# Differential attention inside its projection and its out product, with the head norms split around their roots

## The chip, the cores and the metric

The kernel runs on one core of one Trainium2 chip. The metric is the device time of one execution in microseconds, as the median of the runs. The engines of the core are TensorE (PE; its weight loads are PEld), VectorE (DVE), ScalarE (ACT), GpSimd (POOL) and SyncE (SP, which issues the DMAs). Each works through its own queue in order, and they meet at semaphores.

## The reference, cut to what matters

Two blocks of two layers are computed on 256 tokens of width 1024. The change lies in one layer, the differential attention of the second block. It has 8 heads with two maps each (16 maps), a norm of each map's query and key, a rotation of their first 16 features, two softmaxes per head of which the second is subtracted, and a norm of each head's result before the out product:

```python
def _diff_attention(h, positions, w_qkv, q_gain, k_gain, lam_q1, lam_k1, lam_q2, lam_k2,
                    subln_gain, w_out, lambda_init):
    ...
    qkv = h @ w_qkv
    q, k, v = jnp.split(qkv, 3, axis=-1)
    q = _rmsnorm(q.reshape(B, S, H, 2, Dh), q_gain)
    k = _rmsnorm(k.reshape(B, S, H, 2, Dh), k_gain)
    v = v.reshape(B, S, H, 2 * Dh)
    ...
    q = _partial_rope(q, cos, sin)
    k = _partial_rope(k, cos, sin)
    ...
        p = jax.nn.softmax(s, axis=-1)
        a = (p[:, :, 0] - lam * p[:, :, 1]).astype(v_t.dtype)
        return jnp.einsum('bhqk,bhkd->bhqd', a, v_t)
    ...
    o = (_rmsnorm(o, subln_gain).astype(jnp.float32) * (1.0 - lambda_init)).astype(h.dtype)
    return o.reshape(B, S, H * 2 * Dh) @ w_out
```

## The kernel before

Eight phases follow each other on the core: mixer "ev", mixture of experts "m0", mixer "od", "m1", mixer "sg", dense feed forward "ff", mixer "da" (the differential attention), "m2". All tensors are float32. A projection is made exact enough by splitting each operand into a high and a low part and adding three products (lines 465 to 467); ScalarE makes the high part of a weight piece (`pj_hi`, line 492), VectorE the low part (`pj_lo`, line 502). The order of the work is written out by hand: each engine's queue is the order in which the functions below call it, and nothing else sorts it.

Phase "da" has four steps before the change.

Projection. The weight `w_qkv` of 1024 x 3072 comes in six pieces of 512 columns, two of queries, two of keys, two of values. A piece is multiplied in four quarters (`project_quarter`) of 12 matmuls. A quarter's place in `pj_hi` and `pj_lo` is free once TensorE has used it (`pj_used`), and the next piece's quarter then fills it: a cast on ScalarE, a subtraction on VectorE, which I call a low part. Token tiles 0 and 1 collect in a pair of PSUM banks, three pairs in turn (`da_pair`).

Head norms. For a query or key piece ScalarE squares the banks (line 2764), and VectorE's `da_heads_vector` sums per map, asks GpSimd for the reciprocal root (`rsqrt_vector`, which asks and at once waits; GpSimd's instruction is line 357) and rotates. Later `da_turn_tensor` transposes the piece's result on TensorE (8 transposes, line 2717), a turn. All of VectorE's queue behind `da_heads_vector`, the next piece's low parts too, stands while it waits for the root.

Units. One unit is one map. TensorE makes its logits (lines 2738, 2739), VectorE masks them and takes the maximum (line 674), ScalarE makes the exponentials (652), TensorE transposes them (632), ScalarE copies them out of PSUM (660), TensorE multiplies by the values (640), VectorE divides and, for every second unit, subtracts the pair and sums squares (681, 2877 to 2884). `attention_tensor` and its two partners run the 16 units as a pipeline of three stages: logits of unit u, transposes of u-1, values of u-2. PSUM banks for logits, transposes and outputs are doubled.

Out product. One norm over all 8 heads (2888, root, 2892), 16 transposes of the mix (574), copies with the gain on VectorE (610), and 32 matmuls of 512 columns (587; the profile shows each as two instructions), 8 for each piece `k` of the out weight and each token tile. The first two stages of this, the norm and the transposes, wait for the last unit (`mix_ready`). While TensorE multiplies, VectorE makes the low parts of the first expert's weights. Then VectorE adds the result to `h` (line 600), and phase "m2" begins.

## Time and profile before

| | |
|---|---|
| median of 3 runs | 2301.13 us (2300.80, 2301.13, 2312.22) |
| the profiled execution | 2296.46 us |
| its span, first to last instruction | 2294.7 us |
| TensorE busy, share of the span | 2137.6 us, 93% |
| VectorE busy | 1745.9 us, 76% |
| ScalarE busy | 1429.3 us, 62% |
| phase "da" from the end of its first piece to its last matmul | 1104.6 to 1255.1 us |

A line of the trace names the engine, the line of the kernel, the operation and "out<-in" by the program's names; "arena" is the tensor that holds most of a phase's intermediate results, "bank" is PSUM. The start of each instruction is in microseconds from the start of the span. A matmul's duration reaches over the start of the next one, since they are pipelined, so what one costs is read from one start to the next.

### The profile page before, as it was taken

Reading aid. Unit: us, or ns where it says so; the run is one execution under the profiler, and the core shown is the slowest. Engines: PE = TensorE matmul, PEld = TensorE weight load, DVE = VectorE, ACT = ScalarE, POOL = GpSimd, SP = SyncE. Lnnn points to the kernel's source line nnn. Section 1 sums busy time; section 2 is a strip of 40 time slices with the busy share of each in tenths; the row PEclk is TensorE's granted clock in tenths of the full one; section 3 lists DMA queues with packets and bytes.
Section 4 is the critical chain, followed back from the end, with each engine's and each line's share of the span. In section 5 each row is a group of like instructions: output and inputs, shape, how many; then the busy total and the mean of one; then the engine's idle time right before and its main releaser. Section 6 shows DMA issues by size and latency. Waiting matters only on the chain.

```text
span 2294.7 us, 31436 instructions
## 1 busy us (share of the span) xinstructions
PE 2137.6 (93%) x9970; PEld 1729.8 (75%) x9970; DVE 1745.9 (76%) x2350; ACT 1429.3 (62%) x1919; POOL 76.3 (3%) x71
## 2 busy tenths in 40 slices
PE   8998997997997998999887799999999999999998
PEld 7965776865775886887764687878878787878786
DVE  4755888646887656555664698989899898989897
ACT  5652775443774543444441587877778787878785
POOL 0001000001000000111100000000000000000000
PEclk9998999997998998999998899999999999999999
DMA  6324883423873544542320698989989898989895
GB/s 248 145 80 192 334 330 142 152 112 152 362 273 119 194 185 187 232 169 96 120 111 1 269 383 318 378 315 381 369 331 376 324 373 323 374 322 376 320 386 207
DMA packets 81400, 577.11 MB, mean 251 GB/s; under 512 B 9392, under 2 KB 9392, under 8 KB 12848
## 3 DMA queue, kind: packets, MB, share of 16 engines
q1 hardware_dynamic: 79744, 570.40, 63.3%
q0 software_dynamic: 1584, 5.77, 0.8%
q8 instruction: 43, 0.70, 0.1%
q14 instruction: 29, 0.24, 0.0%
HBM read 575.08 MB, written 1.05 MB: 251 GB/s over the span
## 4 chain that ended last, share of the span: by engine, by line
PE 77%; DVE 12%; issue 5%; ACT 4%; DMA 1%; POOL 1%; DVEq 0%; SPq 0%; ACTq 0%; POOLq 0%
PE bank L465 22%; PE bank L467 21%; PE bank L466 21%; PE bank L587 2%; PE bank L923 2%; PE bank L1396 2%; DVE h L1754 1%; PE bank L1362 1%; DVE gu_lo L1702 1%; DVE pj_lo L502 1%; DVE dn_lo L1702 1%; PE bank L1435 1%; ACT gu_hi L1531 1%; ACT dn_hi L1539 1%; DVE hidt_lo L1702 1%
## 5 line engine op out<-in xcount | busy, mean ns | idle before, releaser
L1702 DVE TENSOR_TENSOR gu_lo<-ffw_gu,gu_hi 128x1024 fp32r<-128x1024 f32 x620 | 755.3, 1238 | 89.7 <-ACT gu_hi L1531 75.0
L1531 ACT CAST gu_hi<-ffw_gu 128x1024 fp32r<-128x1024 f32 x620 | 648.2, 1053 | 102.0 <-PE bank L467 69.1
L465 PE MATMUL bank<-gu_hi,xg_lo 128*128 128x512 f32 x1152 | 462.5, 401 | 5.8 <-DVE xg_lo L1702 4.7
L467 PE MATMUL bank<-gu_hi,xg_hi 128*128 128x512 f32 x1152 | 451.8, 392 | 0.0
L466 PE MATMUL bank<-gu_lo,xg_hi 128*128 128x512 f32 x1152 | 451.1, 392 | 0.0
L1702 DVE TENSOR_TENSOR dn_lo<-ffw_d,dn_hi 128x1024 fp32r<-128x1024 f32 x299 | 362.7, 1222 | 57.4 <-ACT dn_hi L1539 48.0
L1539 ACT CAST dn_hi<-ffw_d 128x1024 fp32r<-128x1024 f32 x310 | 325.3, 1055 | 95.2 <-PE bank L467 91.5
L465 PE MATMUL bank<-dn_hi,hidt_lo 128*128 128x512 f32 x664 | 264.9, 399 | 29.3 <-DVE hidt_lo L1702 29.3
L467 PE MATMUL bank<-dn_hi,hidt_hi 128*128 128x512 f32 x664 | 259.1, 390 | 0.0
L466 PE MATMUL bank<-dn_lo,hidt_hi 128*128 128x512 f32 x664 | 259.0, 390 | 0.0
L465 PEld LDWEIGHTS bank<-gu_hi,xg_lo 128*128 128x128 f32 x1152 | 217.5, 189 | 48.7 <-DVE xg_lo L1702 5.3
L467 PEld LDWEIGHTS bank<-gu_hi,xg_hi 128*128 128x128 f32 x1152 | 217.2, 189 | 46.2
L466 PEld LDWEIGHTS bank<-gu_lo,xg_hi 128*128 128x128 f32 x1152 | 218.1, 189 | 41.5
L502 DVE TENSOR_TENSOR pj_lo<-pieces,pj_hi 128x1024 fp32r<-128x1024 f32 (+2 forms) x108 | 125.3, 1179 | 69.6 <-ACT pj_hi L492 59.6
L492 ACT CAST pj_hi<-pieces 128x1024 fp32r<-128x1024 f32 (+2 forms) x104 | 104.1, 1011 | 112.4 <-PE bank L467 98.2
L465 PEld LDWEIGHTS bank<-dn_hi,hidt_lo 128*128 128x128 f32 x664 | 124.7, 188 | 64.6 <-DVE hidt_lo L1702 24.1
L465 PE MATMUL bank<-pj_hi,xm_lo 128*128 128x512 f32 (+2 forms) x320 | 129.9, 406 | 21.3 <-DVE xm_lo L447 14.2
L467 PEld LDWEIGHTS bank<-dn_hi,hidt_hi 128*128 128x128 f32 x664 | 124.6, 188 | 26.5
L466 PEld LDWEIGHTS bank<-dn_lo,hidt_hi 128*128 128x128 f32 x664 | 124.8, 188 | 24.0
L1561 ACT CAST hidt_hi<-bank 128x256 fp32r<-128x256 f32 x166 | 61.9, 373 | 124.2 <-PE bank L1362 124.2
L467 PE MATMUL bank<-pj_hi,xm_hi 128*128 128x512 f32 (+2 forms) x320 | 125.9, 394 | 0.0
L466 PE MATMUL bank<-pj_lo,xm_hi 128*128 128x512 f32 (+2 forms) x320 | 125.8, 393 | 0.0
(397 smaller groups left out, 2794.7 us busy)
## 6 DMA issues: line engine op xcount, KB each, us to landing
ffw_gu<-in_gate_up_m SPq DMA_DIRECT2D x288, 1024.0 KB, 6.9
ffw_d<-in_down_m SPq DMA_DIRECT2D x144, 1024.0 KB, 7.5
pieces<-in_pieces SPq DMA_DIRECT2D x70, 1024.0 KB, 7.0
ffw_gu<-in_gate_up_ff SPq DMA_DIRECT2D x22, 1024.0 KB, 6.9
ffw_d<-in_down_ff SPq DMA_DIRECT2D x11, 1024.0 KB, 8.9
pieces<-in_pieces SPq DMA_DIRECT2D x4, 512.0 KB, 8.1
norm_vec<-in_ln_g POOLq DMA_DIRECT2D x4, 512.0 KB, 3.9
norm_vec<-in_ln_b POOLq DMA_DIRECT2D x4, 512.0 KB, 5.2
```

Source lines behind the costliest of these rows:

```text
L465: nc.tensor.matmul(bank, a_lo, b_hi, start=start, stop=False)
L466: nc.tensor.matmul(bank, a_hi, b_lo, start=False, stop=False)
L467: return nc.tensor.matmul(bank, a_hi, b_hi, start=False, stop=stop)
L492: nc.scalar.copy(pj_hi[:, 2 * k:2 * k + 2, 0:cols], piece_ap(g)[:, 2 * k:2 * k + 2, :]).then_inc(sem("pj_hi_ready"), 1)
L502: V.tensor_tensor(pj_lo[:, cs, 0:cols], piece_ap(g)[:, cs, :], pj_hi[:, cs, 0:cols].bitcast(F32), ALU.subtract).then_inc(sem("pj_split"), 1)
L587: last = nc.tensor.matmul(psum[2 * j + half], mixT[:, k, c, j * P:(j + 1) * P], wt[:, c, half * 512:(half + 1) * 512], start=(k == 0 and c ...
L923: last = nc.tensor.matmul(psum[2 * j + half], ev_mixT[:, k, c, TILES[j]], piece_ap(even_out[k])[:, c, half * 512:(half + 1) * 512], start= ...
L1396: last = nc.tensor.matmul(psum[5 + half], pick_t[:, j, :], src[:, j, cols], start=(j == 0 and part == 0), stop=(j == T - 1 and part == 1))
L1531: nc.scalar.copy(gu_hi[:, 2 * k:2 * k + 2, :], ffw_gu[:, blk["slot"], 2 * k:2 * k + 2, :])\
L1539: nc.scalar.copy(dn_hi[:, f, :], ffw_d[:, blk["slot"], f, :]).then_inc(sem("down_hi_ready"), 1)
L1561: nc.scalar.copy(hidT_hi[:, st["par"]].rearrange("p f t -> p (f t)"), psum[2][:, st["par"] * BLK:(st["par"] + 1) * BLK]).then_inc(sem("hid ...
L1702: return V.tensor_tensor(out, x, hi.bitcast(F32), ALU.subtract)
```

## The change

Phase "da" is put in another order. The pieces come as query 0, key 0, value 0, query 1, key 1, value 1, so that maps 0 to 7 are complete after three pieces. Their eight units then run between the quarters of pieces 3 to 5: `da_step_tensor(pe, 0, i)` for i from 0 to 9 behind quarters 12 to 21 (`DA_STEP`), with the stages of the pipeline as before. The turns stand behind quarters 6, 11, 20 and 23 (`DA_TURN`). Units 8 to 15 run after the projection, with the 16 matmuls of the first out piece between them in eight parts of two (`DA_OUT_BEHIND`). The head norm of a piece is in two steps, `da_heads_begin_vector` before the root and `da_heads_end_vector` behind it, with two low parts between them. The norm before the out product is made for heads 0 to 3 and heads 4 to 7 apart, each in two steps too. The projection uses two pairs of banks and not three; units use one bank for the transposes (6) and one for the outputs (7, in halves). Three memsets that stood behind the first head norm stand at the head of VectorE's queue.

```diff
-    da = [("qkv", "tok", columns("l1_da_w_qkv_2", 512 * i, 512 * (i + 1)), 512) for i in range(6)]
+    da = [(("q", "k", "v")[i // 2], "tok", columns("l1_da_w_qkv_2", 512 * i, 512 * (i + 1)), 512) for i in (0, 2, 4, 1, 3, 5)]
...
+    DA_STEP = {12 + i: i for i in range(10)}
...
+    def da_step_tensor(pe, first, i):
+
+        if i < 8:
+            u = first + i
+            for g in range(2):
+                pe.wait_ge(sem(f"turned_read{g}"), DA_TURNED + 2 + first // 4)
+            if i >= 2:
+                pe.wait_ge(sem("at_masked"), DA_U0 + u - 1)
+            q, k, bank = (da_q_odd if u % 2 else da_q_even)[:, u // 2, :], da_kT[:, u // 2, :], psum[4 + u % 2]
+            nc.tensor.matmul(bank[:, 0:P], q[:, 0:P], k[:, 0:P], start=True, stop=True)
+            nc.tensor.matmul(bank[:, P:3 * P], q[:, P:S], k, start=True, stop=True).then_inc(sem("at_logits"), 1)
+        if 1 <= i <= 8:
+            u = first + i - 1
+            pe.wait_ge(sem("at_probs"), DA_U0 + u + 1)
+            if u:
+                pe.wait_ge(sem("at_probst"), DA_U0 + u)
+            for b in range(3):
+                last = nc.tensor.transpose(psum[6][:, b * P:(b + 1) * P], da_probs[:, u % 2, b, :], ident)
+            last.then_inc(sem("at_turned"), 1)
+        if i >= 2:
+            u = first + i - 2
+            pe.wait_ge(sem("at_probst"), DA_U0 + u + 1)
...
+            if u:
+                pe.wait_ge(sem("at_written"), DA_U0 + u)
...
+            last.then_inc(sem("at_outputs"), 1)
...
     def da_tensor(pe):
         t = "da"
-        project_first_tensor(pe, t, da_pair(0))
+        project_first_tensor(pe, t, 0)
         for n in range(1, 6):
...
+            for k in range(4):
+                project_quarter(pe, t, n, k, 2 * (n % 2))
+                at = 4 * n + k
+                if at in DA_STEP:
+                    da_step_tensor(pe, 0, DA_STEP[at])
+                if at in DA_TURN:
+                    da_turn_tensor(pe, DA_TURN[at])
...
+        da_mix_turn_tensor(pe, 0)
+        parts = 0
+        for i in range(10):
+            da_step_tensor(pe, 8, i)
+            for _ in range(DA_OUT_BEHIND.count(i)):
...
+                last = da_out_tensor(0, j, half, cs)
+                parts += 1
+        last.then_inc(sem("out_piece"), 1)
+        da_mix_turn_tensor(pe, 1)
...
+        for j in range(T):
+            for half in range(2):
+                last = da_out_tensor(1, j, half, range(4))
+            last.then_inc(sem("out_tile"), 1)
...
     def da_scalar(act):
...
+            for k in range(4):
+                at = 4 * n + k
+                piece_hi_scalar(act, "da", n + 1, (k,))
+                if k == 3:
+                    da_evacuate_scalar(act, n)
+                if at in DA_STEP:
+                    da_step_scalar(act, 0, DA_STEP[at])
+                if at in DA_TURN:
+                    da_turned_scalar(act, DA_TURN[at])
...
+    def da_heads_begin_vector(dve, n):
...
+        root_ask_vector()
+        da_asked[n] = roots["asked"]
+
+    def da_heads_end_vector(dve, n):
+
+        m = DA_MAPS[DA_ROUND[n]]
+        dve.wait_ge(sem("root_found"), da_asked[n])
...
     def da_vector(dve):
+        vlink(V.memset(da_q_even[64:P], 0.0))
+        vlink(V.memset(da_q_odd[0:64], 0.0))
+        vlink(V.memset(at_sums, 0.0))
         for n in range(6):
...
+            for k in range(4):
+                at = 4 * n + k
+                i = DA_STEP.get(at, -1)
+                if at == 12:
+                    da_values_vector(dve, n - 1)
+                if 0 <= i < 8:
+                    da_mask_vector(dve, i)
+                if k == 0 and n - 1 in DA_ROUND:
+                    da_heads_begin_vector(dve, n - 1)
+                piece_lo_vector(dve, "da", n + 1, (k,))
+                if i >= 2:
+                    da_write_vector(dve, i - 2)
+                if i == 9:
+                    da_norm_begin_vector(0)
+                if k == 1 and n - 1 in DA_ROUND:
+                    da_heads_end_vector(dve, n - 1)
+                if at == 22:
+                    da_norm_end_vector(0)
+                if at in DA_TURN:
+                    da_turned_vector(dve, DA_TURN[at])
+        da_values_vector(dve, 5)
+        da_mixed_vector(dve, 0)
+        for i in range(10):
+            if i < 8:
+                da_mask_vector(dve, 8 + i)
+            if i >= 2:
+                da_write_vector(dve, 6 + i)
+        da_norm_begin_vector(1)
+        da_norm_end_vector(1)
+        da_mixed_vector(dve, 1)
```

VectorE's queue at the end of the first piece, before. L502 is a low part, L2785 and L2787 are the norm before its root, L2793 to L2805 the norm behind it and the rotation, and the memsets clear the halves of the query tensors.

```order
L502 TENSOR_TENSOR pj_lo<-pieces,pj_hi 128x1024 x4
L2785 TENSOR_REDUCE arena<-arena 128x16
L2787 TENSOR_SCALAR arena<-arena 128x16
L2793 TENSOR_SCALAR arena<-arena 128x16
L2802 TENSOR_TENSOR arena<-arena,spare 128x16x8
L2803 TENSOR_TENSOR arena<-arena,spare 128x16x8
L2804 TENSOR_TENSOR arena<-arena,spare 128x256
L2805 TENSOR_TENSOR arena<-arena 128x2x8x16
L2867 MEMSET arena 64x2048
L2868 MEMSET arena 64x2048
L2869 MEMSET small 128x32
L502 TENSOR_TENSOR pj_lo<-pieces,pj_hi 128x1024 x4
```

The same place after the change, where the two steps of the norm are lines 2894, 2896 and 2908 to 2920:

```order
L3031 MEMSET arena 64x2048
L3032 MEMSET arena 64x2048
L3033 MEMSET small 128x32
L502 TENSOR_TENSOR pj_lo<-pieces,pj_hi 128x1024 x4
L2894 TENSOR_REDUCE arena<-arena 128x16
L2896 TENSOR_SCALAR arena<-arena 128x16
L502 TENSOR_TENSOR pj_lo<-pieces,pj_hi 128x1024 x2
L2908 TENSOR_SCALAR arena<-arena 128x16
L2917 TENSOR_TENSOR arena<-arena,spare 128x16x8
L2918 TENSOR_TENSOR arena<-arena,spare 128x16x8
L2919 TENSOR_TENSOR arena<-arena,spare 128x256
L2920 TENSOR_TENSOR arena<-arena 128x2x8x16
```

The memsets now stand ahead of the first low parts, and two low parts stand between the sum and what needs the root.

TensorE's queue where the projection ends and the units begin, before. L465 to L467 belong to a quarter, L2717 is a turn, L2738 and L2739 are a unit's logits, L632 its transposes, L640 its products with the values.

```order
L467 MATMUL bank<-pj_hi,xm_hi 128x512
L2717 MATMUL bank<-ident,arena 128x128 x8
L2738 MATMUL bank<-arena 128x128
L2739 MATMUL bank<-arena 128x256
L2738 MATMUL bank<-arena 128x128
L2739 MATMUL bank<-arena 128x256
L632 MATMUL bank<-ident,arena 128x128 x3
L2738 MATMUL bank<-arena 128x128
L2739 MATMUL bank<-arena 128x256
L632 MATMUL bank<-ident,arena 128x128 x3
L640 MATMUL bank<-arena 128x128 x3
```

After the change, TensorE's queue between quarters 13 and 14 (from the last three matmuls of quarter 13), where L2746 are the transposes:

```order
L465 MATMUL bank<-pj_hi,xm_lo 128x512
L466 MATMUL bank<-pj_lo,xm_hi 128x512
L467 MATMUL bank<-pj_hi,xm_hi 128x512
L2738 MATMUL bank<-arena 128x128
L2739 MATMUL bank<-arena 128x256
L2746 MATMUL bank<-ident,arena 128x128 x3
L2759 MATMUL bank<-arena 128x128 x3
L465 MATMUL bank<-pj_hi,xm_lo 128x512
L466 MATMUL bank<-pj_lo,xm_hi 128x512
```

And after the projection, where L2769 are the 8 transposes of half the mix, L2759 the products with the values, and each L2776 is a matmul of the out product:

```order
L2725 MATMUL bank<-ident,arena 128x128 x8
L2769 MATMUL bank<-ident,arena 128x128 x8
L2738 MATMUL bank<-arena 128x128
L2739 MATMUL bank<-arena 128x256
L2776 MATMUL bank<-pieces,arena 128x512 x2
L2738 MATMUL bank<-arena 128x128
L2739 MATMUL bank<-arena 128x256
L2746 MATMUL bank<-ident,arena 128x128 x3
L2776 MATMUL bank<-pieces,arena 128x512 x2
L2738 MATMUL bank<-arena 128x128
L2739 MATMUL bank<-arena 128x256
L2746 MATMUL bank<-ident,arena 128x128 x3
L2759 MATMUL bank<-arena 128x128 x3
L2776 MATMUL bank<-pieces,arena 128x512 x2
```

Units 0 to 7 stand singly between quarters, each step behind 12 matmuls, and units 8 to 15 have parts of the out product between them, which stood behind all units before.

## Rows read from the trace of the kernel before

**Rows 1.** The page: the chain that ended last, its shares by engine.
```profile
PE 77%; DVE 12%; issue 5%; ACT 4%; DMA 1%; POOL 1%; DVEq 0%; SPq 0%; ACTq 0%; POOLq 0%
```

**Rows 2.** Stretches: length, busy (x) of PE, PEld, DVE, ACT, POOL, PEclk, DMA, GB/s.
```profile
1104.60:1174.20 69.60, 61.85 (x273) 50.35 (x272) 44.67 (x59) 30.62 (x38) 11.60 (x4) 0.95 0.42 154
1174.20:1216.80 42.60, 29.61 (x208) 24.56 (x208) 29.75 (x136) 22.20 (x81) 0.00 (x0) 1.00 0.11 46
1216.80:1222.70 5.90, 0.03 (x1) 0.03 (x1) 2.63 (x4) 0.05 (x1) 2.89 (x1) 0.62 0.00 0
1222.70:1226.60 3.90, 3.90 (x17) 3.44 (x18) 2.08 (x3) 3.84 (x4) 0.00 (x0) 0.50 0.02 4
1226.60:1255.10 28.50, 28.50 (x67) 12.61 (x67) 9.91 (x14) 0.00 (x0) 0.56 (x1) 0.97 0.00 0
```

**Rows 3.** Waits, 1104.6 to 1260: who waited for whom: us, times, longest.
```profile
PE bank L632 <- ACT arena L652: 10.6, 9, 1.5
...
PE bank L465 <- DVE pj_lo L502: 6.8, 3, 4.0
DVE arena L2793 <- POOL arena L357: 6.2, 2, 3.1
```

**Rows 4.** Timeline around the second weight piece: start, us, engine, line, [idle before <-releaser].
```profile
1101.66 3.92 DVE L502 TENSOR_TENSOR pj_lo<-pieces,pj_hi 128x1024 fp32r<-128x1024 f32 x3 [2.30 <-ACT pj_hi L492]
...
1108.68 2.91 POOL L357 TENSOR_TENSOR arena<-arena,small 128x16 f32<-128x16 f32 x1 [13.80 <-DVEq L362]
...
1113.97 1.76 DVE L2867 MEMSET arena<- 64x2048 f32 x1 [0.60 <-DVE arena L2805]
...
1119.46 0.79 PE L465 MATMUL bank<-pj_hi,xm_lo 128*128 128x512 f32 x1 [3.99 <-DVE pj_lo L502]
```

**Rows 5.** Timeline, TensorE alone, one attention unit that waits for nothing.
```profile
1186.29 0.39 PE L2738 MATMUL bank<-arena 128*128 128x128 f32 x2
1186.51 0.60 PE L2739 MATMUL bank<-arena 128*128 128x256 f32 x2
1186.94 0.49 PE L632 MATMUL bank<-ident,arena 128*128 128x128 f32 x3
1187.27 0.83 PE L640 MATMUL bank<-arena 128*128 128x128 f32 x6
1187.94 0.39 PE L2738 MATMUL bank<-arena 128*128 128x128 f32 x2
```

**Rows 6.** Timeline, TensorE alone: a quarter's ends, and the transposes of a turn.
```profile
1109.64 0.39 PE L467 MATMUL bank<-pj_hi,xm_hi 128*128 128x512 f32 x1
...
1112.36 0.39 PE L467 MATMUL bank<-pj_hi,xm_hi 128*128 128x512 f32 x1
...
1131.91 1.03 PE L2717 MATMUL bank<-ident,arena 128*128 128x128 f32 x8
1132.70 0.48 PE L465 MATMUL bank<-pj_hi,xm_lo 128*128 128x512 f32 x1
```

**Rows 7.** Busy time of the out product's line alone, 1234 to 1254.
```profile
1234.00:1254.00 20.00, 20.00 (x48) 8.76 (x48) 1.00 0.00 0
```

**Rows 8.** VectorE's groups by line, 1104.6 to 1174.1: xcount, busy us, mean ns.
```profile
L502 DVE TENSOR_TENSOR pj_lo<-pieces,pj_hi 128x1024 fp32r<-128x1024 f32 x18 | 21.2, 1222 | 1.5 <-ACT pj_hi L492 0.7 <-DVE arena L2805 0.2
```

**Rows 9.** GpSimd's root line: xcount: duration ns min/median/max, start us, forms.
```profile
L357 POOL TENSOR_TENSOR small<-small x20: 545/554/1042, 160.9 to 1260.5; 128x1 f32<-128x1 f32 x18, 128x4 f32<-128x4 f32 x1, 128x2 f32<-128x2 f32 x1
L357 POOL TENSOR_TENSOR arena<-arena,small x5: 2894/2896/2907, 1108.7 to 1217.2; 128x16 f32<-128x16 f32 x5
```

**Rows 10.** Timeline: two places where VectorE and GpSimd work side by side.
```profile
892.53 0.55 POOL L357 TENSOR_TENSOR small<-small 128x1 f32<-128x1 f32 x1 [5.61 <-DVEq L362]
892.54 1.25 DVE L1702 TENSOR_TENSOR xt_lo<-xT,xt_hi 128x1024 fp32r<-128x1024 f32 x1
...
1022.54 2.40 POOL L1684 TENSOR_TENSOR dn_lo<-ffw_d,dn_hi 128x1024 fp32r<-128x1024 f32 x1 [14.43 <-ACT dn_hi L1539]
...
1023.86 2.17 DVE L1702 TENSOR_TENSOR gu_lo<-ffw_gu,gu_hi 128x1024 fp32r<-128x1024 f32 x1 [1.49 <-ACT gu_hi L1531]
```

More of the change, by code:

```diff
@@ new lines, in da_mix_turn_tensor, with da_out_tensor @@
+    def da_mix_turn_tensor(pe, k):
+        pe.wait_ge(sem("mix_ready"), 4 + k)
+        for b in range(2):
+            for i in range(4):
+                c, j = 2 * b + i // 2, i % 2
+                last = nc.tensor.transpose(psum[4 * k + b][:, i * P:(i + 1) * P],
+                                           da_mix[:, j, 512 * k:512 * (k + 1)].rearrange("t (p c) -> t c p", c=4)[:, c, :], ident)
+            last.then_inc(sem("mixt_turned"), 1)
+    def da_out_tensor(k, j, half, cs):
+        for c in cs:
+            last = nc.tensor.matmul(psum[2 * j + half], da_mixT[:, k, c, TILES[j]],
+                                    piece_ap(da_out[k])[:, c, half * 512:(half + 1) * 512],
+                                    start=(k == 0 and c == 0), stop=(k == 1 and c == 3))
+        return last
@@ L2734, in da_tensor @@
[L2734 to L2742 removed]
+                read_wait(pe, t, 0, n - 1)
@@ new lines, in da_norm_begin_vector, with da_norm_end_vector @@
+    def da_norm_begin_vector(k):
+        vlink(V.tensor_scalar(da_hs_flat[k], da_hs_flat[k], RMS_EPS, None, ALU.add))
+        root_ask_vector()
+    def da_norm_end_vector(k):
+        root_wait_vector()
+        for j in range(T):
+            y = da_mix[:, j, 512 * k:512 * (k + 1)].rearrange("p (h d) -> p h d", d=P)
+            vlink(V.scalar_tensor_tensor(out=y, in0=y, scalar=1.0 - LAMBDA_INIT, in1=over(da_hs[:, k, j, :], 2, P),
+                                         op0=ALU.mult, op1=ALU.mult), *([sem("mix_ready")] if j else []))
@@ new lines, in da_turned_vector, with da_values_vector @@
+    def da_turned_vector(dve, o):
+        dve.wait_ge(sem("da_qk_turned"), 2 * o + 2)
+        for dst, src, gain in da_turned_parts(DA_MAPS[o], 1):
+            last = V.tensor_scalar(dst, src, gain, None, ALU.mult)
+        last.then_inc(sem("turned_read1"), 1)
+    def da_values_vector(dve, n):
+        full_wait(dve, "da", 1, n)
+        vlink(V.tensor_scalar(da_v[:, 1, 512 * (n // 3):512 * (n // 3 + 1)], psum[2 * (n % 2) + 1], rstd[:, 1:2], None,
+                              ALU.mult), sem("bank1_read"))
```

223 lines of the change are left out of this document (122 added, 101 removed).

## Prediction

> **What bounds the kernel now.** I read four things, in this order. First the chain that ended last, by engine [rows 1]: 77% of the span is TensorE, so what shortens the time is work or idle time on TensorE's queue. Second, busy time by stretch of the phase that the change touches [rows 2]. The reader is to see that TensorE works 61.85 of 69.6 us in the projection, 29.61 of 42.6 us in the units, nothing in the 5.9 us of the norm, and that its clock is 0.50 in the 3.9 us of transposes behind that idle time. The five stretches make 150.5 us, from 1104.6 (the end of the first weight piece) to 1255.1 (the last matmul). Third, who waits for whom [rows 3]: in the units TensorE waits for ScalarE's exponentials, nine waits that the profile names with 10.6 us in all; in the projection it waits for VectorE's low parts, 6.8 us, and VectorE stands for a root, 3.1 us each time. Fourth, the timeline of the second piece [rows 4]: the root runs from 1108.68 for 2.91 us, then come the rotation and, from 1113.97, the memsets, and TensorE has idled 3.99 us when its low part is there at 1119.46. VectorE is no bound here: 44.67 of 69.6 and 29.75 of 42.6 us. The idle time comes from the order of the queues.
>
> **Prices.** A quarter is 12 matmuls, from 1109.64 to 1112.36, 2.72 us [rows 6]. A turn moves the next matmul from 1131.91 to 1132.70, 0.8 us [rows 6]. A unit that waits for nothing costs TensorE 1.65 us, from its logits at 1186.29 to the next at 1187.94: 0.65 logits, 0.33 transposes, 0.67 values [rows 5]. The same unit took 42.6 / 16 = 2.66 us as the units stood [rows 2]. The out product's row counts 48 instructions in 20 us at full clock and 64 (two for each of 32 matmuls) fill 28.5 us at 0.97 [rows 7, 2]: 0.417 to 0.445 each; I take 0.43, so 0.86 a matmul and 1.7 for a part of two.
>
> **The sum, from the end of the first piece.** I walk the new queues in their order with these prices.
>
> Projection. 20 quarters, 54.4. Four turns, 3.2. Units 0 to 7 now lie between quarters, 8 x 1.65 = 13.2 on TensorE. What each needs of VectorE and ScalarE was asked for a whole slot (2.72 + 1.65 = 4.4 us) earlier, and a unit's work there is 29.75 / 16 = 1.86 and 22.20 / 16 = 1.39 us [rows 2] beside a low part of 1.22 [rows 8], so it is hidden; without that cover a slot would cost the 1.0 us more (2.66 - 1.65) that it cost before. A low part is made a piece ahead of its use, which is four slots: no wait either. Waits that stay: the two memsets of 1.76 us with their gaps of some 0.5 take 4.1 us where VectorE idled 2.30 [rows 4], so the first low part ends near 1104.8 and TensorE waits 0.3. The turn of query 0: VectorE makes the second of two low parts after the second quarter (1104.9 + 5.4 = 1110.3, then ScalarE's cast, put at a low part's 1.22 [rows 8], and the low part, 2.4), then the rotation, 1.8 as from the root's end at 1111.6 to the memset's idle time of 0.60 before 1113.97 [rows 4], ready at 1114.5 to 1114.9; TensorE comes at 1113.1 and waits 1.8. The other turns have more room; between 0 and 3 x 1.8 I take 0.9, near the lower end, since two of them stand two quarters and more behind their rotation. One short stretch at the lower clock after it, 0.7. Projection with eight units: 54.4 + 3.2 + 13.2 + 3.0 + 0.7 = 74.5.
>
> Between. A wait of 0.6 (an estimate, the width of one multiplication of half the mix) for the first half's norm, whose root of 8 columns lies beside other work, and 8 transposes, 0.9, as a turn: 1.5.
>
> Second units and first out piece. Step 0: 0.65 logits, 1.4 until VectorE has copied the transposed half (two copies of 0.69, as 2.08 for three [rows 2]), a part 1.7. Step 1: 0.65 + 0.33 + 1.7. Steps 2 to 4: 1.65 + 1.7 = 3.35 each, more than the 2.66 of the loop through the other engines, so TensorE sets them: 10.1. Steps 5 to 7 have no part: 2.66 each, 8.0. Step 8: 1.0 + 1.7 and 0.7, as the loop still runs through the other engines. Step 9: 0.67 + 3.4. In all 32.1. The eight units and the first out piece alone took 21.3 + 14.2: this place gives 3.4 us only, for two thirds of the idle time of a unit is not covered by a part.
>
> Tail. Before, 5.9 us lay between the last unit and the transposes [rows 2]. The root has 8 columns; 4 took 1.04 and 16 took 2.90 [rows 9], so between these, I take 1.7 and save 1.2. The two multiplications have half the width, 1.1 less. With the last unit's own division and squares (1.9, an estimate; a whole unit is 1.86 on average) it makes 5.5 to 6, of which the last two parts cover 3.4: 2.4. Eight transposes at the lower clock, half of 3.9, are 1.95, the copy behind them 1.35, 16 matmuls 13.7, and 1.2 for the lower clock at their start, as before. 20.6.
>
> Hand-offs that such a sum leaves out, 0.8. Total 74.5 + 1.5 + 32.1 + 20.6 + 0.8 = 129.5, against 150.5: **21 us less**. The queues of SyncE and GpSimd gain no DMA and one root; a piece is asked for when the low parts two before it are done, and slots that grow longer give it more time. ScalarE loads as many activation tables in the new list of instructions as in the old. What follows in phase m2 waits for this phase's end and moves with it. The profiled execution took 2296.46 us, 1.8 more than its span, and would take 2275.5; the median of the runs is 4.7 above it, so I predict 2280.0.
>
> **A rule against it.** The split norm puts a root of 2.90 us beside low parts. Where GpSimd subtracted 1024 columns from 1022.54 for 2.40 us, VectorE's low part, begun at 1023.86, took 2.17 us instead of 1.22: it stood until GpSimd was done. Beside a root of 0.55 us at 892.53, however, one took 1.25, begun 0.01 later [rows 10]. If the four long roots did block as the subtraction did, the low part behind each would start up to 2.9 us later, of which the wait for its quarter hides a part; only where a turn follows soon does it count. Ahead of the first turn the two low parts would end at 1112.8 and 1113.9 (the root's end at 1111.6, then 1.22 and 1.1) and the rotation at 1115.9, 1.1 later; the other turns, with more room, I put at 0.6 together. That is 1.7 us, so 2281.7. I give it 0.12. The Trainium skill, page "SBUF — State Buffer", section "SBUF: two separate sides", states that the port pair that VectorE and GpSimd share is an exclusive lock held for the whole instruction, so that the other fully blocks when a VectorE operation with two SBUF inputs meets one of GpSimd. By that rule the time is 2281.7. The subtraction's rows agree with it, the short root's do not.
>
> **Rivals.**
> - The queues' order costs what it saves: each of the ten slots and eight later steps waits for a hand-off, because masks stand behind low parts and exponentials behind casts. For it: nine such waits in the units now, up to 1.5 us. Against it: the slot of 4.4 us. At 0.5 us in 18 places the gain is 12, time 2289; at 1.0, which is the old cost, 3 and 2298. Chance 0.15 for the first and 0.04 for the second.
> - Slower: TensorE's clock. If the mix of short matmuls and waits let it fall to the lower of its levels (1.2 GHz) from the first unit on, units 0 to 7 (13.2), the ten quarters between them (27.2), units 8 to 15 (13.2) and the parts (13.7) would cost twice, up to 67 more. It decides from 21 us of such work at half clock on, where the gain is gone. For it: 0.50 behind the idle 5.9 us. Against it: 1.00 through all units, with TensorE busy 29.61 of 42.6, less than it will be [rows 2]. Half of the second group at half clock gives 2293; all of it and the slots give 2347. Chance of an end slower than before 0.02.
> - The change doesn't do what it says, since the phase behind waits for something else than this phase (a weight that lands at a fixed time): within 0.5% of before, 2301. Against it: DMA share is 0.00 behind 1216.8 [rows 2], so nothing is under way that it could wait for. Chance 0.02.
>
> **How the numbers follow.** Forecast (75 to 80 quarters and units hidden, 18 to 24 us gained) 0.65, the lock 0.12, hand-offs 0.15 and 0.04, clock 0.02, nothing 0.02. A difference of 0.5%, 11.5 us, is about what a measurement of this kernel can tell from none. Faster by more than that: 0.65 + 0.12 + 0.15 = 0.92; same 0.04 + 0.02; slower 0.02. The range is 2272 to 2289: its low end has the turns free of waits (2.7), no lower clock in the tail (2.2) and a tail of 1 us less, and 2 us for the spread of the runs; its high end the first case of the hand-offs.
>
> **What the profile will show.** The five stretches' total falls from 150.5 to about 130. TensorE's idle time up to the end of the projection is below 5 us, the largest piece before the first turn; the waits for low parts are gone; the root lies beside a low part, and if that low part takes 1.22 the lock is wrong. Quarters with a unit start 4.4 us apart. In the second group five steps are 3.4 us apart and three 2.7. Before the last transposes there is one wait of 2 to 3 us, and the clock is at 0.50 in them. Wrong it would be with waits for exponentials in every slot, or with a granted clock below 0.9 over the whole stage.

## Result and profile after

| | before | after |
|---|---|---|
| median of 5 runs | 2301.13 us (2300.49 to 2312.22) | 2284.39 us (2279.54 to 2285.40) |
| the profiled execution, its span | 2296.46, 2294.7 us | 2285.40, 2283.7 us |
| TensorE busy | 2137.6 us, 93% | 2142.7 us, 94% |
| end of the first piece to the last matmul | 150.5 us | 131.9 us |

The ratio of the times is 0.9921, 95% interval [0.9907, 0.9934]: 18.2 us less by the ratio. 21 were predicted; 2284.4 lies in the range. The page's lines of busy time and of the chain by engine, which answer to [rows 1]:

```profile
PE 2142.7 (94%) x9970; PEld 1734.1 (76%) x9970; DVE 1748.5 (77%) x2353; ACT 1429.6 (63%) x1919; POOL 77.7 (3%) x72
...
PE 78%; DVE 11%; issue 5%; ACT 4%; DMA 1%; DVEq 0%; POOL 0%; SPq 0%; ACTq 0%; POOLq 0%
```

The phase from the end of its first piece on, cut at the places where the prediction's sum was cut: projection with units 0 to 7, the first transposes of the mix, second units with parts, wait and last transposes with their copy, last 16 matmuls. The columns are those of [rows 2], busy time of TensorE, its weight loads, VectorE, ScalarE and GpSimd, then clock, DMA share and GB/s:

```profile
1110.14:1187.99 77.85, 73.97 (x376) 61.87 (x376) 57.79 (x127) 41.75 (x78) 14.27 (x5) 0.98 0.37 137
1187.99:1189.60 1.61, 1.04 (x10) 1.07 (x10) 1.46 (x3) 0.29 (x1) 0.00 (x0) 1.00 0.82 285
1189.60:1220.98 31.38, 28.15 (x138) 18.19 (x136) 16.79 (x72) 10.89 (x40) 1.13 (x1) 1.00 0.12 50
1220.98:1225.43 4.45, 1.52 (x9) 1.14 (x9) 2.91 (x5) 2.41 (x3) 0.50 (x1) 0.81 0.00 0
1225.43:1241.97 16.54, 16.54 (x34) 7.24 (x35) 9.03 (x12) 1.48 (x2) 0.56 (x1) 0.84 0.00 1
```

TensorE now has 73.97 us of work in 77.85, where it had 61.85 in 69.6. The clock column reads 0.81 and 0.84 in the last two stretches; part of the 2.4 us by which 131.9 misses the prediction's 129.5 lies there. TensorE's waits up to 1188, and those behind it; they answer to [rows 3]:

```profile
PE bank L2725 <- DVEq L296: 3.1, 3, 2.4
PE bank L465 <- DVE pj_lo L502: 0.8, 1, 0.8
...
PE bank L2769 <- DVEq L296: 2.6, 2, 2.1
PE bank L2746 <- ACT arena L2845: 2.2, 3, 1.1
PE bank L2776 <- issue: 1.0, 1, 1.0
PE bank L2776 <- DVE arena L3027: 0.9, 1, 0.9
```

The nine waits for exponentials (10.6 us) and the three for low parts (6.8 us) of before are gone; one of 0.8 for a low part, behind the memsets, is left. The 2.2 us at L2746 are new in kind: L2845 is ScalarE's copy that frees the one bank of the transposes, and TensorE waits for it in three steps, all without a part in front (1209.21, 1212.20 and 1213.76). Between quarters no wait of a unit is on the list. TensorE's timeline shows the slots, by the first logits of three units that follow each other in the projection, and then the steps of the second group, two with a part and two without:

```profile
1153.62 0.38 PE L2738 MATMUL bank<-arena 128*128 128x128 f32 x2
...
1158.02 0.38 PE L2738 MATMUL bank<-arena 128*128 128x128 f32 x2
...
1162.42 0.38 PE L2738 MATMUL bank<-arena 128*128 128x128 f32 x2
...
1199.32 0.39 PE L2738 MATMUL bank<-arena 128*128 128x128 f32 x2
...
1202.69 0.38 PE L2738 MATMUL bank<-arena 128*128 128x128 f32 x2
...
1206.07 0.38 PE L2738 MATMUL bank<-arena 128*128 128x128 f32 x2
1207.72 0.39 PE L2738 MATMUL bank<-arena 128*128 128x128 f32 x2
...
1210.24 0.39 PE L2738 MATMUL bank<-arena 128*128 128x128 f32 x2
```

Slots are 4.40 us apart (4.4 predicted), steps with a part 3.37 (3.35), and the steps without one 1.65 and then 2.52 (2.66: the first of them lives on the lead that the parts had given the other engines).

The first turn is where most was missed. TensorE's last matmul before it, the turn's eight transposes, and the matmuls behind:

```profile
1119.00 0.39 PE L467 MATMUL bank<-pj_hi,xm_hi 128*128 128x512 f32 x1
1121.78 1.97 PE L2725 MATMUL bank<-ident,arena 128*128 128x128 f32 x8 [2.39 <-DVEq L296]
1123.40 0.78 PE L465 MATMUL bank<-pj_hi,xm_lo 128*128 128x512 f32 x1
...
1124.40 0.58 PE L467 MATMUL bank<-pj_hi,xm_hi 128*128 128x512 f32 x1
1124.81 0.40 PE L465 MATMUL bank<-pj_hi,xm_lo 128*128 128x512 f32 x1
```

It waits 2.39 us instead of 1.8, and then the matmuls start 0.43 apart instead of 0.23 until 1124.8: the lower level of the clock. Why it waits longer stands on VectorE and GpSimd. First VectorE's low parts beside the first two roots, then GpSimd's roots:

```profile
1115.89 1.23 DVE L502 TENSOR_TENSOR pj_lo<-pieces,pj_hi 128x1024 fp32r<-128x1024 f32 x1 [0.15 <-DVE arena L2896]
...
1131.23 1.28 DVE L502 TENSOR_TENSOR pj_lo<-pieces,pj_hi 128x1024 fp32r<-128x1024 f32 x1
```

```profile
1115.94 3.94 POOL L357 TENSOR_TENSOR arena<-arena,small 128x16 f32<-128x16 f32 x1 [15.44 <-DVEq L362]
1131.22 2.90 POOL L357 TENSOR_TENSOR arena<-arena,small 128x16 f32<-128x16 f32 x1 [11.34 <-DVEq L362]
...
1183.45 1.63 POOL L357 TENSOR_TENSOR arena<-arena,small 128x8 f32<-128x8 f32 x1 [2.97 <-DVEq L362]
```

The second root began 0.01 us before its low part, and both ran at their length (2.90; 1.28 for 1.22). The first began 0.05 us behind its low part and took 3.94, 1.04 more; the rotation stood until 1119.9 for it. So one engine did hold the other up here, but the other way round than in the prediction's rival; root_first tests it.

**Outside the stretch.** The phase's first matmul stood at 1088.7 us before and at 1094.3 after, though nothing ahead of it was changed, and from the last addition to `h` to the end of the span it was 1039.7 and 1041.7. Over all profiles shown below these two lengths lie between 1088.6 and 1097.1, and 1038.9 and 1043.2, with no order by kernel. The two profiled executions are also an unequal pair: that of before, 2296.46 us, is below all five timed ones, and that of the changed kernel, 2285.40, is the slowest of its five. So the experiments are compared by the phase itself, from its first matmul to the start of VectorE's addition of token tile 1 to `h` (166.4 before, 147.7 after), and the whole by the timed ratio.

### The profile page after: what moved, and what is told of

It is laid out like the page before. It is cut to its first block, busy times and chain, and to the rows that moved or that the text cites. A ratio compares the mean times of both kernels' runs of the same rounds, so it can differ in the third digit from the quotient of the medians.

```text
span 2283.7 us, 31475 instructions
## 1 busy us (share of the span) xinstructions
PE 2142.7 (94%) x9970; PEld 1734.1 (76%) x9970; DVE 1748.5 (77%) x2353; ACT 1429.6 (63%) x1919; POOL 77.7 (3%) x72
## 4 chain that ended last, share of the span: by engine, by line
PE 78%; DVE 11%; issue 5%; ACT 4%; DMA 1%; DVEq 0%; POOL 0%; SPq 0%; ACTq 0%; POOLq 0%
PE bank L465 22%; PE bank L467 21%; PE bank L466 21%; PE bank L923 2%; PE bank L1396 2%; DVE h L1754 1%; PE bank L1362 1%; PE bank L587 1%; PE bank L2776 1%; DVE gu_lo L1702 1%; DVE dn_lo L1702 1%; DVE pj_lo L502 1%; PE bank L1435 1%; ACT gu_hi L1531 1%; ACT dn_hi L1539 1%
## 5 line engine op out<-in xcount | busy, mean ns | idle before, releaser
L465 PE MATMUL bank<-gu_hi,xg_lo 128*128 128x512 f32 x1152 | 462.9, 402 | 5.0 <-DVE xg_lo L1702 4.5
L467 PE MATMUL bank<-gu_hi,xg_hi 128*128 128x512 f32 x1152 | 452.2, 393 | 0.0
L465 PE MATMUL bank<-dn_hi,hidt_lo 128*128 128x512 f32 x664 | 265.7, 400 | 29.2 <-DVE hidt_lo L1702 29.2
L467 PE MATMUL bank<-dn_hi,hidt_hi 128*128 128x512 f32 x664 | 259.6, 391 | 0.0
L465 PEld LDWEIGHTS bank<-gu_hi,xg_lo 128*128 128x128 f32 x1152 | 217.6, 189 | 48.5 <-DVE xg_lo L1702 5.3
L467 PEld LDWEIGHTS bank<-gu_hi,xg_hi 128*128 128x128 f32 x1152 | 217.4, 189 | 46.4
L502 DVE TENSOR_TENSOR pj_lo<-pieces,pj_hi 128x1024 fp32r<-128x1024 f32 (+2 forms) x108 | 126.1, 1180 | 74.2 <-ACT pj_hi L492 64.5
L465 PEld LDWEIGHTS bank<-dn_hi,hidt_lo 128*128 128x128 f32 x664 | 125.1, 188 | 64.7 <-DVE hidt_lo L1702 24.1
L467 PEld LDWEIGHTS bank<-dn_hi,hidt_hi 128*128 128x128 f32 x664 | 125.0, 188 | 26.7
L465 PE MATMUL bank<-pj_hi,xm_lo 128*128 128x512 f32 (+2 forms) x320 | 130.8, 409 | 15.3 <-DVE xm_lo L447 14.2
L467 PE MATMUL bank<-pj_hi,xm_hi 128*128 128x512 f32 (+2 forms) x320 | 125.9, 394 | 0.0
```

The costliest lines, as they stand in the source:

```text
L465: nc.tensor.matmul(bank, a_lo, b_hi, start=start, stop=False)
L467: return nc.tensor.matmul(bank, a_hi, b_hi, start=False, stop=stop)
L502: V.tensor_tensor(pj_lo[:, cs, 0:cols], piece_ap(g)[:, cs, :], pj_hi[:, cs, 0:cols].bitcast(F32), ALU.subtract).then_inc(sem("pj_split"), 1)
```

## Experiments

The phase in four parts, us, from starts in TensorE's timeline: from the phase's first matmul to the second turn, to the mix's first transposes, to its last ones, to the addition to `h`. Ratios are to the kernel before; where two intervals overlap, only the profile tells the kernels apart, and it is one execution. Timed executions of one kernel lie up to 11.8 us apart (parts_single, 2274.20 to 2285.98), the slower at a lower granted clock (0.965 against 0.969 and 0.970), and where the others lost it isn't recorded. The profile of root_first is the fastest of its four, that of parts_last the slowest of its four (2291.97, with two at 2283).

| kernel | to 2nd turn | to mix | to last | to `h` | phase | ratio, 95% |
|---|---|---|---|---|---|---|
| changed | 44.1 | 50.2 | 34.5 | 19.0 | 147.7 | 0.9921 [0.9907, 0.9934] |
| after_again | 44.1 | 50.2 | 34.5 | 19.0 | 147.7 | 0.9922 [0.9901, 0.9942] |
| norms_whole | 41.0 | 65.3 | 34.7 | 17.9 | 158.9 | 0.9958 [0.9942, 0.9973] |
| units_behind | 43.7 | 64.2 | 35.1 | 16.2 | 159.2 | 0.9978 [0.9966, 0.9989] |
| parts_last | 44.2 | 50.2 | 41.0 | 16.1 | 151.5 | 0.9926 [0.9903, 0.9949] |
| root_first | 41.7 | 50.2 | 34.5 | 16.2 | 142.6 | 0.9894 [0.9873, 0.9915] |
| memsets_gpsimd | 42.3 | 50.2 | 34.5 | 17.9 | 144.8 | 0.9909 [0.9896, 0.9923] |
| turn_later | 40.1 | 50.2 | 34.5 | 19.2 | 144.0 | 0.9906 [0.9891, 0.9921] |
| parts_four | 44.1 | 50.2 | 34.5 | 16.1 | 144.9 | 0.9908 [0.9893, 0.9923] |
| filled_wait | 44.1 | 50.2 | 34.5 | 16.2 | 145.0 | 0.9902 [0.9887, 0.9917] |
| parts_single | 43.7 | 50.1 | 31.4 | 16.1 | 141.4 | 0.9889 [0.9866, 0.9913] |
| all_three | 38.9 | 50.2 | 31.4 | 16.1 | 136.6 | 0.9872 [0.9850, 0.9894] |

A trap lies in the first column. Up to the second turn units_behind and parts_single run the same instructions as the changed kernel, but from the first to the last matmul start of the first piece they took 18.57 and 18.55 us, where the changed kernel and six others with the same instructions there took 15.44 to 15.56 in eight profiles. The first piece in the changed kernel, then in parts_single:

```profile
1094.30:1110.14 15.84, 13.82 (x56) 10.97 (x56) 11.18 (x19) 4.39 (x5) 1.11 (x2) 0.90 0.16 68
```

```profile
1092.26:1111.20 18.94, 16.92 (x57) 13.46 (x58) 12.85 (x20) 4.38 (x5) 1.11 (x2) 0.75 0.14 58
```

The clock is 0.90 and 0.75. The 3.1 us come back in part, since the low parts are then in time and the root comes first (see root_first), which leaves 43.7 for 44.1. So a difference of a microsecond or two in that column can be the clock's and not the edit's.

### norms_whole: the split of the head norms undone

```diff
 if k == 0 and n - 1 in DA_ROUND:
     da_heads_begin_vector(dve, n - 1)
+    da_heads_end_vector(dve, n - 1)
...
-if k == 1 and n - 1 in DA_ROUND:
-    da_heads_end_vector(dve, n - 1)
```

> The head norm of a piece back in one step: behind the root's request VectorE waits for the root and rotates, before any low part; all else as in the changed kernel, whose stretch from the end of the first piece (1110.14) to the last matmul (1242.0) is 131.9 us. Theory (the split carries part of the gain, because in a slot of 4.4 us VectorE has 1.22 of low part and 1.86 of the unit to do, and a stand of 2.9 for the root with 1.8 of rotation doesn't fit beside them): the two norms that lie among the units make TensorE wait 4 to 5 us each, the stretch grows by 8 to 10, to about 141, ratio to the kernel before 0.996. Rival (low parts are made a piece ahead, so the stand is covered and the split is worth nothing): 132 to 134, ratio 0.992 to 0.993.

The theory's ratio and its waits; the phase grew by 11.2 us, a little above its 8 to 10. One of the two waits stands on TensorE, and what VectorE did meanwhile:

```profile
1165.98 1.62 PE L2759 MATMUL bank<-arena 128*128 128x128 f32 x6 [4.56 <-DVEq L296]
1167.25 0.77 PE L465 MATMUL bank<-pj_hi,xm_lo 128*128 128x512 f32 x1
```

```profile
1162.12 0.17 DVE L2908 TENSOR_SCALAR arena<-arena 128x16 f32<-128x16 f32 x1 [3.06 <-POOL arena L357]
...
1164.01 1.23 DVE L502 TENSOR_TENSOR pj_lo<-pieces,pj_hi 128x1024 fp32r<-128x1024 f32 x1
...
1165.35 0.42 DVE L2985 TENSOR_TENSOR arena<-bank,small 128x256 f32<-128x256 f32 x1
```

TensorE waits 4.56 us (and 4.34 at the other norm) for the division of a unit's output, which frees the bank and stands in VectorE's queue behind root, rotation and low part. The stretch to the mix grew by 15.1: 8.9 in these two waits, 1.1 at the first logits, most of the rest at the lower clock behind them (1.62 for a group that takes 0.83). Without the split 11.2 of the phase's 18.7 us are gone, and about half of the gain by the ratio. Ahead of the slots, though, the whole norm costs nothing (41.0 against 44.1).

### units_behind: no units between the quarters

```diff
-DA_STEP = {12 + i: i for i in range(10)}
+DA_STEP = {}
...
+for i in range(10):
+    da_step_tensor(pe, 0, i)
 da_mix_turn_tensor(pe, 0)
```

> Units 0 to 7 run behind the projection and not between its quarters; the norm of heads 0 to 3 then stands open behind them too. All else as in the changed kernel. Theory (a unit costs TensorE 1.65 us between quarters and 2.66 in a row): 8 x 1.0 = 8 us, and some 6 us for the norm that nothing covers any more: the stretch of 131.9 grows to 146, ratio 0.998. Rival (the hand-offs cost in the slots what they cost in a row, the gain is from the norms and parts): growth by the norm's 6 us alone, 138, ratio 0.995.

ScalarE's and VectorE's steps, and the norm of heads 0 to 3, move behind the projection too. From the second turn on, with the last part left out, it is 99.3 against 84.7 us, 14.6 more: the theory's 14, and far from the rival's 6. The whole phase grew by 11.5, since the last part ran at full clock here (16.2 for 19.0). Of TensorE's groups in 1174 to 1202, the transposes of a unit waited 5.7 us for exponentials and copies, and those of the mix 5.5 for the norm:

```profile
L2744 PE MATMUL bank<-ident,arena 128*128 128x128 f32 x24 | 4.2, 282 | 5.7 <-ACT arena L2845 4.4 <-ACT arena L2837 1.2
...
L2767 PE MATMUL bank<-ident,arena 128*128 128x128 f32 x1 | 0.5, 489 | 5.5 <-DVEq L296 5.5
```

### parts_last: the first out piece behind all units

```diff
-DA_OUT_BEHIND = (0, 1, 2, 3, 4, 8, 9, 9)
+DA_OUT_BEHIND = (9, 9, 9, 9, 9, 9, 9, 9)
```

> All eight parts of the first out piece behind step 9 of the second units, none between them. Theory (a part between units fills about 1 us of idle time of a step, while idle time before the last transposes costs twice, as wait and as lower clock behind it): five parts cost 1.7 instead of 0.7, 5.0 more; the wait of 2.1 us before the last transposes goes, and with it the lower clock in them and in the last 16 matmuls (0.6 and 2.7). The stretch stays within 1.5 us of 131.9, ratio 0.992. Rival (the clock's loss at the end isn't due to the wait): 134.5 to 135, ratio 0.993, granted clock behind the parts about 0.8 as now.

Half right. The last stretch fell from 19.0 to 16.1, at full clock, as the theory has it; but the one before grew by 6.5, and the sum by 3.7, where the theory allowed 1.5. The clock was lost in two other places instead, behind a wait of 2.03 us in the first steps and behind waits of 1.89 and 0.37 in the last (the first two rows); behind the parts it was 1.00 (the third), so the rival falls:

```profile
1193.00:1197.00 4.00, 1.97 (x11) 1.55 (x10) 2.60 (x10) 1.92 (x9) 0.00 (x0) 0.87 0.81 338
1211.00:1218.00 7.00, 5.18 (x25) 4.69 (x26) 2.97 (x14) 2.19 (x8) 0.00 (x0) 0.65 0.01 2
...
1234.50:1248.60 14.10, 14.04 (x35) 6.42 (x36) 9.11 (x13) 0.00 (x0) 0.56 (x1) 1.00 0.00 0
```

The timed ratio can't tell it from the changed kernel, and this profile is the slowest of its four executions, so what a kernel with all parts last costs as a rule stays open.

### root_first: the first root begins ahead of the low part

```diff
 root_ask_vector()
+if n == 0:
+    vlink(V.memset(rope_both, 0.0))
```

> One memset of 128x256 on VectorE between the request of the first head norm's root and the low part behind it, so that the root begins before the low part and not 0.05 us behind it. Theory (a 128x16 root holds no low part up, but waits for one that began earlier: 3.94 instead of 2.90 us): the root takes 2.90, the low part beside it 1.28, and TensorE's wait before the first turn falls from 2.39 to about 1.6. Rival (this root is long for another reason, such as GpSimd's 15 us without work): it takes 3.9 again and the wait stays 2.4.

GpSimd, and VectorE beside it:

```profile
1110.20 2.91 POOL L357 TENSOR_TENSOR arena<-arena,small 128x16 f32<-128x16 f32 x1 [15.42 <-DVEq L362]
```

```profile
1110.24 0.27 DVE L2900 MEMSET arena<- 128x256 f32 x1 [0.24 <-DVE arena L2896]
1110.54 1.22 DVE L502 TENSOR_TENSOR pj_lo<-pieces,pj_hi 128x1024 fp32r<-128x1024 f32 x1
1112.10 1.22 DVE L502 TENSOR_TENSOR pj_lo<-pieces,pj_hi 128x1024 fp32r<-128x1024 f32 x1 [0.34 <-ACT pj_hi L492]
```

The root takes 2.91 behind the same 15.4 us without work, so the rival falls; the low part inside it and the one that begins inside it take 1.22 each. All profiles agree: in the six where the first root began 0.05 or 0.06 us behind a low part it took 3.94, in the five where it began 0.28 us or more ahead of it, 2.91. Two of these five, units_behind and parts_single, have no edit there. TensorE's wait is 1.46 instead of 2.39. Behind it the turn took no half clock, so the stretch to the second turn fell by 2.4 and not by 0.9. The last stretch fell too, by 2.7, with the same wait of 2.06 us before it, which nobody expected; see below.

### memsets_gpsimd, turn_later: the first turn's two waits

```diff
+if phase == 6:
+    pool.wait_ge(sem("root_found"), roots["answered"])
+    pool.memset(da_q_even[64:P], 0.0).then_inc(sem("da_zeroed"), 1)
+    pool.wait_ge(sem("da_zeroed"), 1)
+    pool.memset(da_q_odd[0:64], 0.0).then_inc(sem("da_zeroed"), 1)
+    pool.wait_ge(sem("da_zeroed"), 2)
...
-vlink(V.memset(da_q_even[64:P], 0.0))
-vlink(V.memset(da_q_odd[0:64], 0.0))
```

> The two large memsets on GpSimd, at the head of its part of the phase, instead of VectorE. Theory: VectorE's first low part is in time, TensorE's wait of 0.79 us before the second piece is gone, the stretch of 131.9 falls by 0.8 and the stage starts no later. The first root still waits about 1 us if a low part begins first. Rival (GpSimd's memsets hold VectorE's subtractions for the last xm_lo up, as its 1024-column subtraction did): TensorE's wait in the first piece grows by 1 us or more and nothing is gained.

The wait of 0.79 is gone and VectorE isn't held up: GpSimd's second memset ran from 1103.02 for 1.80, and VectorE's two subtractions for `xm_lo`, begun at 1104.25, took 1.29 for both, as without it. The low part here came 0.33 us behind the root, which took 2.91, and the first turn waited 1.45. Against that a lower clock in the first piece cost about 1.4, since without it the stretch would be root_first's 41.7 less 0.8, and it was 42.3.

```diff
-DA_TURN = {6: 0, 11: 1, 20: 2, 23: 3}
+DA_TURN = {7: 0, 11: 1, 20: 2, 23: 3}
```

> The first turn stands behind quarter 7 instead of 6. Theory (its wait of 2.39 us is for the rotation, which is ready 1121.7, before quarter 7 would end, and the half clock in the turn and the quarter behind it comes from that wait): the wait goes, the eight transposes take 0.95 instead of 1.62, the quarter 2.72 instead of 3.2; the stretch falls by 3.0 to 3.6, to about 128.6. Rival (VectorE's later copy pushes the next norm and the wait comes back before the second turn): the second turn waits 2 us instead of 0.44 and less than 1.5 us is gained.

To the second turn 4.0 us less, a little over the theory; the second turn's wait is 0.44 as it was, so the rival falls.

### parts_four, filled_wait: the clock at the end

```diff
-DA_OUT_BEHIND = (0, 1, 2, 3, 4, 8, 9, 9)
+DA_OUT_BEHIND = (0, 1, 2, 3, 9, 9, 9, 9)
```

> Parts behind steps 0, 1, 2, 3, 9, 9, 9, 9 instead of 0, 1, 2, 3, 4, 8, 9, 9. Theory: 6.9 us of parts cover the last unit's division, the norm's root and the multiplications (5.5 us), so that TensorE doesn't idle before the last transposes and its clock stays at the full level: the part taken from step 4 costs 1.0 more, the wait of 2.06 goes, and the lower clock's 3.3 us (0.6 in the transposes, 2.7 in the last 16 matmuls) too; the stretch falls by 3 to 4.5, to 128. Rival (the clock falls at the end of the stage whatever TensorE did before): a fall of 1.0 only, granted clock about 0.8 in the last 16 matmuls.

```diff
 last.then_inc(sem("out_piece"), 1)
+for _ in range(2):
+    nc.tensor.matmul(psum[6], da_mixT[:, 0, 0, TILES[0]], piece_ap(da_out[0])[:, 0, 0:512], start=True, stop=True)
 da_mix_turn_tensor(pe, 1)
+nc.tensor.matmul(psum[6], da_mixT[:, 0, 0, TILES[0]], piece_ap(da_out[0])[:, 0, 0:512], start=True, stop=True)
```

> Three matmuls of 512 columns whose result nobody reads are added: two in the wait before the last eight transposes, one in the wait for their copy (added work, nothing of the result depends on it). Theory (the clock at the end is lost through TensorE's 2 us without work): the granted clock stays 1.00, the transposes take 0.95 instead of 1.52, the last 16 matmuls 13.7 instead of 16.4, and the stretch falls by about 3, though work was added. Rival (the clock is lost for another reason): the stretch stays at 131.9 or grows by 0 to 0.5.

Both theories fit, with 2.8 and 2.7 us less (parts_four just below its bound of 3), but each rests on one profile, and two of the kernels that keep the wait kept the clock as well (root_first, units_behind). What carries it is the count: with a wait of 2.06 five of seven profiles lost the clock behind it, without one none of five did. The timed executions agree in kind: clock 0.969 to 0.970 in parts_four and 0.968 to 0.970 in filled_wait, against 0.965 to 0.970 in the changed kernel. The last stretch of filled_wait, with one of its three added matmuls in it, and that of turn_later, which has the wait of 2.06 before it:

```profile
1224.84:1241.07 16.23, 16.10 (x44) 7.64 (x45) 10.45 (x15) 3.86 (x4) 0.56 (x1) 1.00 0.00 0
```

```profile
1221.20:1240.40 19.20, 18.21 (x42) 8.50 (x43) 10.46 (x14) 3.87 (x4) 0.56 (x1) 0.82 0.00 0
```

Same stretch, clock 1.00 and 0.82. In parts_four the stretch before stayed 34.5: the wait that it saved is what the part taken from step 4 costs. All of its gain is clock.

### after_again, parts_single, all_three

> The changed kernel itself once more, profiled anew beside the next ones. What is meant to be the same: from the first matmul of the phase (which stood at 1094.3) to the second turn 44.1 us, from there to the first transposes of the mix 50.2, to the last ones 34.5. What may differ, if the clock's fall behind a wait of some 2 us is a matter of chance and not of this kernel: the last part, 19.0 us here, was 16.2 in two kernels with the same wait of 2.06 (root_first, units_behind) and 17.9, 17.9 and 19.2 in three others. And the phase's start, 1088.6 to 1097.1 in the profiles so far. Theory: the last part is between 16.2 and 19.2 and the first wait (2.4) costs its half clock again. Rival (the loss belongs to this order of work): 19.0 again within 0.2.

As the rival had it: 18.97 both times, and 44.1 to the second turn. But both profiles are among the slow executions of this kernel (2285.40 is the highest of five, 2287.07 the second highest of six, the lowest is 2279.54), so what the faster ones lost isn't shown.

```diff
-DA_OUT_BEHIND = (0, 1, 2, 3, 4, 8, 9, 9)
+DA_OUT_BEHIND = (0, 1, 2, 3, 4, 5, 6, 7, 8, 9, 9, 9, 9, 9, 9, 9)
...
-j, half, cs = 1 - parts // 4, parts // 2 % 2, ((0, 1), (2, 3))[parts % 2]
+j, half, cs = 1 - parts // 8, parts // 4 % 2, (parts % 4,)
```

> The first out piece in sixteen parts of one matmul instead of eight of two: one behind each of steps 0 to 8, seven behind step 9. Theory (a step of 2.66 us has 1.0 us without work and a part of one matmul is 0.86, so it costs nothing, where a part of two costs 0.7; seven matmuls, 6.0 us, cover the last unit's way to the transposes): from the mix's first transposes to the end 47.3 us, against 53.4 in the changed kernel and 50.6 in parts_four; ratio 0.989. Rival (the hand-offs of a step lie in series with the part, as the idle time isn't where the part stands): steps of 3.0 and more, 50 us and more, no better than parts_four.

47.5 us from the mix on, as the theory had it (47.3). Steps on TensorE's timeline, by their first logits:

```profile
1191.89 0.38 PE L2738 MATMUL bank<-arena 128*128 128x128 f32 x2
...
1205.47 0.38 PE L2738 MATMUL bank<-arena 128*128 128x128 f32 x2
```

Five steps lie between them, 13.58 / 5 = 2.72 us each with a part of one matmul in it, against 2.66 for a unit before. Nothing waits before the last transposes.

all_three joins the edits of memsets_gpsimd, turn_later and parts_single.

> The two memsets on GpSimd, the first turn behind quarter 7 and sixteen parts of one matmul, together. Theory (the three don't touch each other): 39.3 us to the second turn (40.1 in turn_later, less the 0.8 of the memsets), 50.2 to the mix, 47.3 from there, 136.8 in all against 147.7; ratio 0.987, some 11 us faster than the changed kernel. Rival (what is saved in the first part comes back as a wait before the second turn, whose norm stands behind VectorE's work): 2 us less of it, ratio 0.988.

136.6 against 136.8 expected; the three add up. All of TensorE's waits from the first piece's end on:

```profile
PE bank L2782 <- issue: 1.0, 1, 1.0
PE bank L2782 <- DVE arena L3033: 1.0, 1, 1.0
PE bank L2752 <- ACT arena L2851: 0.9, 3, 0.4
PE bank L2731 <- DVEq L296: 0.7, 2, 0.4
PE bank L2775 <- DVEq L296: 0.6, 1, 0.6
```

4.2 us are left of the changed kernel's 10.6. At a median of 2273.87 us against 2301.05 for the kernel before, it is the fastest here; its interval, [0.9850, 0.9894], ends below that of the changed kernel.

## Why the prediction was right, and where it missed

**What bounds the kernel.** Idle time from the order of the queues: right. Each of the two parts of the change that could be undone with clear effect, the units in the slots and the split norms, gives back what its waits cost (norms_whole, units_behind).

**The sum**, predicted and measured in the same cuts:

- Projection with eight units: 74.5, measured 77.85, the term that was mis-sized. The wait behind the memsets was 0.79 for 0.3, the first turn's 2.39 for 1.8, the other turns' 0.71 (0.44 and 0.27) for 0.9. The low clock behind the first turn was put at 0.7 and cost 1.45: root_first is 2.38 us shorter to the second turn, of which 0.93 is the wait. That makes 1.6. The rest of 1.7 is, with waits and lower clock taken out, 2.1 more in the 20 quarters (2.83 behind a unit for 2.72, mostly because the first start of a quarter is 0.31 long instead of 0.23, 0.42 behind the first logits), 0.4 more in the turns and 0.8 less in the units. A quarter's price was read from a place with nothing between the quarters, and 0.8 was put for all hand-offs of the phase.
- Between: 1.5, measured 1.61.
- Second units with parts: 32.1, measured 31.38.
- Tail: 20.6, measured 4.45 + 16.54 = 20.99. The wait was 2.06 for 2.4 and transposes with copy 2.39 for 3.3; but the 16 matmuls took 16.54 for 14.9, so that the total is near because errors cancel. At full clock all from the transposes on takes 16.2 instead of 19.0 (root_first, filled_wait).

131.9 instead of 129.5 in all, so 18.6 us gained there instead of 21. In the profiled executions 7.6 of them don't appear in the difference of spans (11.0), since this one reached the phase 5.6 us later and spent 2.0 more behind it. The medians, 16.7 apart, are the better witness.

**The rule against it.** The rival was that a long root holds low parts up. It doesn't, in all profiles: a low part begun 0.01 us behind the root took 1.28, and two begun inside it 1.22 each (root_first). The reverse was not among the prediction's cases: behind a low part begun 0.05 us before it a root took 3.94 for 2.90, about as much more (1.04) as the low part still had to run (1.18); root_first shows the cause by taking it away. The Trainium skill, page "SBUF — State Buffer", section "SBUF: two separate sides", lets whichever of the two starts first keep the shared ports for its whole instruction. The 3.94 us agree with it; the low parts inside a root don't.

**The rivals.** Hand-offs in the slots: none seen, slots of 4.40 us. Clock from the first unit on: no, 1.00 through slots and steps; what it cost, it cost behind waits of about 2 us. The phase behind moved along, so "nothing" fell too; its premise was misread by a little, as [rows 2] have a DMA share of 0.02 at 1222.7 to 1226.6 and not 0.00 throughout. That halving the norm before the out product pays by itself was not tested: units_behind shows a wait of 5.5 us for the first half's norm where nothing covers it, and no kernel has the norm whole.

**What would show it.** Total, slots and the wait before the last transposes came as said, and the waits for low parts are gone but for one of 0.8. Of the first five steps, each with a part, three are 3.4 us apart, as said, the others 3.65 and 2.70 (1189.60 to 1193.25 to 1195.95). The clock in the last transposes was 0.74 (1223.04 to 1224.6) and not 0.50. Idle time to the projection's end was 3.9 us of the 5 allowed, the largest at the first turn.

## What to carry to other kernels

A unit whose hand-offs leave TensorE idle for 1 us costs nothing of that between pieces of a projection, if the slot is longer than what every other engine must do in it (here VectorE was busy 33.95 of the 46 us from 1141 to 1187); then no engine may stand for an answer inside a slot, so ask before and collect a slot later. Fill work is best cut as small as the idle time: one matmul of 0.86 us in each step was all but free (2.72 for 2.66), two cost 0.7. Price a wait of about 2 us on TensorE above its length, since the lower clock behind it may cost as much again (where it came, 1.4 to 3.0 us here; behind the 2.06 us it came in five of seven profiles), and give a small turn one more quarter of room if it has the choice.
